# Differential attention in a two-model transformer kernel: three pairs of score banks, and attention maps combined before they are normalized

## The reference, cut to what matters

```python
lam = exp(sum(lam_q1 * lam_k1)) - exp(sum(lam_q2 * lam_k2)) + lam_init
for i in range(S // BLOCK):                      # 4 blocks of 128 queries
    n_k = (i + 1) * BLOCK
    s = einsum('bqhcd,bkhcd->bhcqk', q[:, i*BLOCK:n_k], k[:, :n_k]) * D ** -0.5
    s = where(kpos <= qpos, s, -inf)
    p = softmax(s, axis=-1)                      # two maps, c = 0 and c = 1
    a = p[:, :, 0] - lam * p[:, :, 1]
    outs.append(einsum('bhqk,bkhe->bqhe', a, v[:, :n_k]))
o = rms_norm(concatenate(outs, axis=1), sub_gain) * (1.0 - lam_init)   # EPS = 1e-6 inside the root
```

## Time and profile before

| | us |
|---|---|
| median of three runs | 3162.12 |
| lowest, highest | 3160.61, 3165.22 |
| profiled execution, its own time | 3168.31 |
| its span in the trace | 3166.3 |
| the differential attention in it, from the last projection matmul to the first matmul behind it | 133.7 (1515.7 to 1649.4) |

### The profile page before, as it was taken

One profiled execution on the slowest core, in us unless ns is written; L12 is line 12 of the kernel. 1 busy time (PEld: TensorE's weight loads), 2 busy tenths in 40 slices (PEclk: granted clock), 3 DMA queues, 4 the chain that ended last, 5 costly groups with the idle time before them and its releaser, 6 DMA issues.

```text
span 3166.3 us, 40442 instructions
## 1 busy us (share of the span) xinstructions
PE 2945.4 (93%) x13848; PEld 2410.2 (76%) x13848; DVE 1786.9 (56%) x2233; ACT 1211.5 (38%) x1940; POOL 1097.6 (35%) x474
## 2 busy tenths in 40 slices
PE   5989999999788999999779999999899998899999
PEld 3767778877566888888458888888887897788887
DVE  7565758474795644666566333667265736663333
ACT  2564432233333422244453222366444654332221
POOL 3311444443103444444214444444302441044443
PEclk7999999998898999999889999999899999999999
DMA  5343445442002333333003333332201330033332
GB/s 193 88 146 127 148 133 196 146 146 61 27 1 67 99 96 97 92 95 87 14 14 99 93 93 97 91 94 87 60 1 51 92 90 11 10 97 93 95 98 93
DMA packets 364856, 278.83 MB, mean 88 GB/s; under 512 B 13362, under 2 KB 320947, under 8 KB 363699
## 3 DMA queue, kind: packets, MB, share of 16 engines
q1 hardware_dynamic: 363472, 276.76, 28.5%
q10 hardware_dynamic: 1251, 0.33, 0.0%
HBM read 274.96 MB, written 2.10 MB: 88 GB/s over the span
## 4 chain that ended last, share of the span: by engine, by line
PE 60%; issue 6%; DVE 6%; ACT 2%; POOL 0%; DVEq 0%; ACTq 0%; POOLq 0%
PE banks L943 12%; PE banks L938 12%; PE banks L947 12%; PE banks L895 6%; PE banks L901 6%; PE banks L898 5%; PE banks L870 1%; DVE Z L2278 1%; PE banks L1180 1%; PE banks L1248 1%; DVE small L2233 1%; PE banks L940 1%; ACT tmp L1742 0%; PE banks L1228 0%; DVE head_sums L2347 0%
## 5 line engine op out<-in xcount | busy, mean ns | idle before, releaser
L772 POOL TENSOR_TENSOR w_lo<-w_raw,w_hi 128x1024 fp32r<-128x1024 f32 (+1 forms) x424 | 1045.6, 2466 | 1904.0 <-ACT w_hi L1375 1902.6
L1375 ACT ACTIVATE w_hi<-w_raw 128x1024 fp32r<-128x1024 f32 (+1 forms) x424 | 445.6, 1051 | 1132.6 <-PE banks L947 830.7
L895 PE MATMUL banks<-w_hi,h_hi 128*128 128x512 f32 x960 | 386.9, 403 | 10.5 <-ACT h_hi L1552 7.2
L898 PE MATMUL banks<-w_hi,h_lo 128*128 128x512 f32 x960 | 378.4, 394 | 3.7 <-DVE h_lo L510 3.7
L901 PE MATMUL banks<-w_lo,h_hi 128*128 128x512 f32 x960 | 378.8, 395 | 0.8 <-POOL w_lo L772 0.7
L938 PE MATMUL banks<-h_hi,w_hi 128*128 128x512 f32 x1280 | 340.8, 394 | 10.0 <-ACT h_hi L1559 9.8
L943 PE MATMUL banks<-h_lo,w_hi 128*128 128x512 f32 x1280 | 318.7, 390 | 1.1 <-DVE h_lo L510 1.1
L938 PEld LDWEIGHTS banks<-h_hi,w_hi 128*128 128x128 f32 x1280 | 243.0, 190 | 66.5 <-issue 14.7
L947 PE MATMUL banks<-h_hi,w_lo 128*128 128x512 f32 x1152 | 284.5, 389 | 0.0
L943 PEld LDWEIGHTS banks<-h_lo,w_hi 128*128 128x128 f32 x1280 | 240.2, 188 | 54.0 <-DVE h_lo L510 4.4
L947 PEld LDWEIGHTS banks<-h_hi,w_lo 128*128 128x128 f32 x1152 | 216.2, 188 | 44.9
(11 more groups left out here) (295 smaller groups left out, 4692.3 us busy)
## 6 DMA issues: line engine op xcount, KB each, us to landing
w_raw<-in_m_w_up SPq DMA_DIRECT2D x64, 512.0 KB, 3.9
w_raw<-in_m_w_down SPq DMA_DIRECT2D x64, 512.0 KB, 3.4
Z<-in_ada_w SPq DMA_DIRECT2D x48, 512.0 KB, 4.8
w_raw<-in_kv_w SPq DMA_DIRECT2D x48, 512.0 KB, 3.7
w_raw<-in_ffn_w_gate SPq DMA_DIRECT2D x44, 512.0 KB, 3.8
w_raw<-in_ffn_w_up SPq DMA_DIRECT2D x44, 512.0 KB, 3.8
tmp<-in_ada_w SPq DMA_DIRECT2D x32, 512.0 KB, 4.7
w_raw<-in_ffn_w_down SPq DMA_DIRECT2D x32, 512.0 KB, 3.4
```

The lines of the kernel that those rows point to most:

```text
L772: pool.tensor_tensor(wlo[j][:, 0:n], raw[j][:, 0:n], whi[j][:, 0:n], ALU.subtract).then_inc(s_wlo, 1)
L895: pe.matmul(t, hh, wh, start=k == 0, stop=False)
L898: pe.matmul(t, hl, wh, start=False, stop=False)
L1375: act.activation(whi[par][:, 0:kc * P], raw[par][:, 0:kc * P], ACT.Copy).then_inc(s_whi, 1)
```

## The change

- **Banks and order.** `diff_scores` takes three pairs of banks (0 to 5). TensorE issues scores(0) and scores(1) ahead of the loop and scores(s + 2) in iteration s, ahead of turn_map(s - 3). The wait in scores(s) is for the exponentials of slot s-3, so scores(s + 2) waits for those of slot s-1. VectorE does neg_max(s + 1) in iteration s, ahead of combine(s - 1). ScalarE's loop still does take_map(s - 3) and then probs(s); its scale moves to the first slot of the next head, ahead of take_map, and y_high to the third slot, behind probs.
- **One bank for transposed maps.** All maps are turned into bank 6 (before: 4 and 5 in turn), so turn_map(s) waits until map s-1 is taken. The mean square goes into bank 6 too (before: bank 7), so mean_square waits until the map just turned has been taken, and the next turn_map waits for the Ln that reads it. Values go into bank 7 (before: 6). mean_square stands behind turn_map in its iteration.
- **Combination.** The first map plus the second times a ratio, -lambda l1/l2, where l1 and l2 are the row sums: a reciprocal and a scalar_tensor_tensor on 128x1 and one scalar_tensor_tensor on the map (before: a reciprocal on 128x2 and two operations on the map). The map is left larger by l1; since it is normalized by its mean square afterwards, only EPS has to be scaled: VectorE computes 128 EPS l1^2 once a head (`scale_eps`, 128x4), and TensorE adds it into the mean square with four float32 matmuls of 128 columns a head.
- **Start of the stage.** ScalarE makes the high parts of head 0, VectorE zeroes the unused halves of head 0's key tiles and makes its low parts; GpSimd zeroes those of head 1 and makes the high parts of heads 1 to 7. TensorE waits for GpSimd's zeroing at slot 4 only.

The diff, cut to its core (a line of "..." marks what is left out):

```diff
 def diff_scores(s, c):
-    return bank[2 * (s % 2) + c]
+    return bank[2 * (s % 3) + c]
...
+def diff_eps(s, n=1):
+    return sums8[:, 28 + s % 8:28 + s % 8 + n]
...
     def diff():
-        for h in range(8):
+        for h in range(1, 8):
+            pool.wait_ge(e["high_parts"], past(3 * h))
             pool.wait_ge(e["scores"], past(NB * (h - 1)))
             pool.tensor_copy(q_hi[h % 2], zt(h)).then_inc(e["high_parts"], 1)
             for c, (r, t) in enumerate(zip(HALF, k_hi)):
...
+        if kind == "diff":
+            todo = [qk[64:128, 5 * S:6 * S], qk[64:128, 7 * S:8 * S], qk[0:64, 9 * S:10 * S], qk[0:64, 11 * S:12 * S]]
...
         def scores(s):
...
             pe.wait_ge(e["low_parts"], past(3 * h + 3))
-            pe.wait_ge(e["probs"], past(2 * s - 2))
+            if s == NB:
+                zero_rows_in(4)
+            pe.wait_ge(e["probs"], past(2 * s - 4))
             qh, ql = (t[h % 2][:, b * P:n] for t in (q_hi, q_lo))
             for c in range(2):
...
         def turn_map(s):
...
             pe.wait_ge(e["combined"], past(s + 1))
-            pe.wait_ge(e["taken"], past(s - 1))
+            pe.wait_ge(e["taken"], past(s))
+            pe.wait_ge(e["log_mean"], past((s + BEHIND - NB) // NB))
             for kb in range(b + 1):
-                mm = pe.transpose(bank[4 + s % 2][:, kb * P:(kb + 1) * P], diff_probs(s, 0)[:, kb * P:(kb + 1) * P], ident)
+                mm = pe.transpose(bank[6][:, kb * P:(kb + 1) * P], diff_probs(s, 0)[:, kb * P:(kb + 1) * P], ident)
             mm.then_inc(e["turned"], 1)
...
         def values(h):
...
             for kb in range(NB):
-                mm = pe.matmul(bank[6][:, kb * P:S], zt(16 + h)[:, kb * P:(kb + 1) * P], zt(24 + kb)[:, kb * P:S],
+                mm = pe.matmul(bank[7][:, kb * P:S], zt(16 + h)[:, kb * P:(kb + 1) * P], zt(24 + kb)[:, kb * P:S],
                                start=kb == 0, stop=kb == NB - 1, skip_group_check=True)
             mm.then_inc(e["values_added"], 1)
...
         def mean_square(h):
             pe.wait_ge(e["squares"], past(h + 1))
-            pe.wait_ge(e["log_mean"], past(h))
-            pe.matmul(bank[7], ones, zt(28), start=True, stop=True).then_inc(e["mean_square"], 1)
+            pe.wait_ge(e["taken"], past(min(NB * h + 2 * NB - BEHIND, DIFF_SLOTS)))
+            pe.wait_ge(e["eps_scaled"], past(h + 1))
+            pe.matmul(bank[6], ones, zt(28), start=True, stop=False, skip_group_check=True)
+            for s in range(NB * h, NB * h + NB):
+                _, b = diff_slot(s)
+                mm = pe.matmul(bank[6][:, b * P:(b + 1) * P], diff_eps(s).to_broadcast([P, P]), ident, start=False, stop=s == NB * h + NB - 1, skip_group_check=True)
+            mm.then_inc(e["mean_square"], 1)
+        scores(0)
+        scores(1)
         for s in range(DIFF_SLOTS + BEHIND):
-            if s < DIFF_SLOTS:
-                scores(s)
+            if s + 2 < DIFF_SLOTS:
+                scores(s + 2)
             h, i = divmod(s, NB)
-            if i == NB - 1 and h:
-                mean_square(h - 1)
             if s >= BEHIND:
                 turn_map(s - BEHIND)
+                if i == NB - 1 and h:
+                    mean_square(h - 1)
                 if i == (BEHIND - 1) % NB and h:
                     values(h - 1)
         mean_square(7)
...
         def probs(s):
...
             act.wait_ge(e["neg_max"], past(s + 1))
             act.wait_ge(e["turned"], past(s - 3))
+            act.wait_ge(e["eps_scaled"], past(h - 1))
             for c in range(2):
-                act.activation(diff_probs(s, c)[:, 0:n], diff_scores(s, c)[:, 0:n], ACT.Exp, bias=diff_small(s, 0)[:, c:c + 1],
-                               accum_out=diff_small(s, 1)[:, c:c + 1]).then_inc(e["probs"], 1)
+                act.activation(diff_probs(s, c)[:, 0:n], diff_scores(s, c)[:, 0:n], ACT.Exp, bias=diff_neg_max(s)[:, c:c + 1],
+                               accum_out=diff_sums(s)[:, c:c + 1]).then_inc(e["probs"], 1)
...
         def scale(h):
...
-            act.activation(zt(29), bank[7], ACT.Ln, bias=eps, scale=1.0 / P).then_inc(e["log_mean"], 1)
+            act.activation(zt(29), bank[6], ACT.Ln, scale=1.0 / P).then_inc(e["log_mean"], 1)
...
+        q_hi, _, k_hi, _ = parts("diff")
+        act.activation(q_hi[0], zt(0), ACT.Copy).then_inc(e["high_parts"], 1)
+        for r, t in zip(HALF, k_hi):
+            act.activation(t[0][r, :], zrows(r, 8), ACT.Copy).then_inc(e["high_parts"], 1)
         for s in range(DIFF_SLOTS + BEHIND):
             h, i = divmod(s, NB)
             if i == NB - 1 and h:
                 square(h - 1)
+            if i == 0 and h >= 2:
+                scale(h - 2)
             if s >= BEHIND:
                 take_map(s - BEHIND)
             if s < DIFF_SLOTS:
                 probs(s)
-            if i == NB - 1 and h:
-                scale(h - 1)
-            if i == 1 and h >= 2:
+            if i == 2 and h >= 2:
                 y_high(h - 2)
...
+        def first_parts():
+            for par in range(2):
+                rows = qk[HALF[1 - par], (4 + 4 * par) * S:(8 + 4 * par) * S].rearrange("p (t n) -> p t n", n=2 * S)[:, :, 0:S]
+                dve.memset(rows.bitcast(F32), 0.0)
+            low_q(0)
+            for c in range(2):
+                low_k(0, c)
         def neg_max(s):
...
         def combine(s):
             h, b = diff_slot(s)
             n = (b + 1) * P
             first, second = (diff_probs(s, c)[:, 0:n] for c in range(2))
-            inv = diff_small(s, 2)
+            ratio, inv = diff_ratio(s)
+            l1, l2 = (diff_sums(s)[:, c:c + 1] for c in range(2))
             dve.wait_ge(e["probs"], past(2 * s + 2))
-            dve.wait_ge(e["combined"], past(s - 3))
-            dve.reciprocal(inv, diff_small(s, 1)).then_inc(e["inverted"], 1)
+            dve.wait_ge(e["combined"], past(s - 1))
+            dve.reciprocal(inv, l2).then_inc(e["inverted"], 1)
             dve.wait_ge(e["inverted"], past(s + 1))
-            dve.tensor_scalar(second, second, inv[:, 1:2], lamv, ALU.mult, ALU.mult).then_inc(e["second_scaled"], 1)
-            dve.wait_ge(e["second_scaled"], past(s + 1))
-            dve.scalar_tensor_tensor(first, first, inv[:, 0:1], second, ALU.mult, ALU.subtract).then_inc(e["combined"], 1)
+            dve.scalar_tensor_tensor(ratio, inv, minus_lam, l1, ALU.mult, ALU.mult).then_inc(e["ratio"], 1)
+            dve.wait_ge(e["ratio"], past(s + 1))
+            dve.scalar_tensor_tensor(first, second, ratio, first, ALU.mult, ALU.add).then_inc(e["combined"], 1)
+        def scale_eps(h):
+            l1 = diff_sums(NB * h, NB).rearrange("p (s c) -> p c s", c=2)[:, 0, :]
+            dve.wait_ge(e["probs"], past(2 * NB * h + 2 * NB))
+            dve.wait_ge(e["mean_square"], past(h - 1))
+            dve.scalar_tensor_tensor(diff_eps(NB * h, NB), l1, P * EPS, l1, ALU.mult, ALU.mult).then_inc(e["eps_scaled"], 1)
...
-            dve.scalar_tensor_tensor(ytile[:, :], bank[6], subg, zt(30), ALU.mult, ALU.mult).then_inc(e["normed"], 1)
+            dve.scalar_tensor_tensor(ytile[:, :], bank[7], subg, zt(30), ALU.mult, ALU.mult).then_inc(e["normed"], 1)
...
-        low_q(0)
-        low_k(0, 0)
-        low_k(0, 1)
+        first_parts()
+        neg_max(0)
         for s in range(DIFF_SLOTS + 1):
             h, i = divmod(s, NB)
-            if s < DIFF_SLOTS:
-                neg_max(s)
+            if s + 1 < DIFF_SLOTS:
+                neg_max(s + 1)
             if s:
                 combine(s - 1)
-            if i == 0 and h >= 2:
+            if i == 0 and h:
+                scale_eps(h - 1)
+            if s == 0:
+                low_q(1)
+                low_k(1, 0)
+            if i == 0 and h < 7:
+                low_k(h + 1, 1)
+            if i == 1 and h >= 2:
                 sub_norm(h - 2)
-            if i == 1 and h < 7:
-                low_q(h + 1)
-            if i >= 2 and h < 7:
-                low_k(h + 1, i - 2)
-            if i == 2 and h >= 2:
+            if i == 2 and h < 6:
+                low_q(h + 2)
+            if i == 3 and h < 6:
+                low_k(h + 2, 0)
+            if i == 3 and h >= 2:
                 sub_low(h - 2)
+        sub_norm(6)
         sub_low(6)
         sub_norm(7)
         sub_low(7)
```

More of the change, by code:

```diff
@@ L136, in program @@
         small = sb("small", [P, 64])
-        lamv = small[:, 0:1]
+        minus_lam = small[:, 0:1]
         m2 = small[:, 48:48 + 4 * GROUPS]
@@ L414, in program @@
                         ("high_parts", "low_parts", "values_in", "block_scores", "reduced", "neg_max", "diagonal", "scores", "probs", "values_added", "inverted", "output", "output_high", "output_low", "max_spread", "sink_or_denominator", "squares_or_taken")}
```

(27 more changed lines are left out.)

6 lines of the change are left out of this document (3 added, 3 removed).

## The result

The changed kernel takes 3193.44 us (median of 4 runs, 3188.40 to 3196.59) against 3163.67 us for the kernel before (4 runs, 3160.61 to 3166.82): ratio 1.0091, 95% interval 1.0074 to 1.0108. It is slower, by 29.8 us between the medians; the forecast was +19.5 us and 3181.6 us, with a range of 3164 to 3194. The profiled execution took 3196.59 us, with a span of 3194.8.

What follows compares the result with a forecast made beforehand. No engine is full, so waits bound the stage. Start -2.8, first eight slots +3.5, five middle heads +19.0 and tail -0.2 give +19.5 us on the median 3162.1: 3181.6 us, range 3164 to 3194.

Steps and rivals of the forecast that it cites:

- The order closes a chain of one lap per slot: TensorE and ScalarE wait on each other every slot; laps sum to 15.7 us a head against 13.66, +9.0 in five heads.
- the sign of being right: Copies wait for transposes and scores for exponentials in nearly every slot, stops near 2 us, values over 4 us in most heads.
- The clock falls once a head: TensorE drops to its lower clock level in every head, 2.0 us each; five heads with laps and falls: +19.0 us.
- The first eight slots: Stage's opening slots, 26.93 us before: 28.4 by laps, +1.5, and +3.5 us with one clock fall.
- Start: Stage start, 8.70 us before: ScalarE casts beside VectorE's zeroing, so 5.9 us from the last projection matmul, -2.8 us.
- Added matmuls: Four matmuls of 128 columns a head on TensorE, with the mean square: 0.9 us, bounds 0 to 2.2.
- Tail: End of the stage, 28.57 us before: 24.4, or 28.4 with two clock falls, -0.2 us.
- The clock holds: Rival: the same laps in the stage without clock falls, +3.5 us, 3165.6 us; chance 0.15.
- It falls twice a head, or once but for double length: Rival: 2 us more in five heads and the first eight slots, +31.5 us, 3193.6 us; chance 0.15.
- The lead survives: Rival: exponentials finish before TensorE reaches scores(s+2), so TensorE's work decides, 11.7 us a head; -17.5 us, 3144.6; chance 0.10.
- Nothing much moves: Rival: part of the ring is unseen slack, and the time stays within 5 us; chance 0.05.

Runs made afterwards that it cites:

- filler: The changed kernel plus five unread bf16 matmuls of 512 columns into bank 6 at the places where TensorE would stop; 3169.7 us.
- norm_fill2: The changed kernel with turn_map(s-3) ahead of scores(s+2), sub_norm a slot earlier, and three overwritten matmuls into bank 7 ahead of the values; 3149.6 us.
- turn_first_norm: The changed kernel with turn_map(s-3) ahead of scores(s+2) on TensorE, and sub_norm, sub_low and y_high each a slot earlier; 3161.8 us.
- probs_first: The changed kernel with ScalarE doing probs(s) ahead of take_map(s-3), TensorE's order unchanged; 3163.8 us.
- old_order: The changed kernel with banks, waits and order of the kernel before, keeping the change's start, combination and EPS matmuls; 3164.3 us.

## Why the prediction was right, and where it was off

- **The order closes a chain of one lap per slot: right.** The predicted laps, 3.53, 2.99, and 15.7 a head, measured 3.55 (1611.90 to 1615.45), 2.94 (1597.22 to 1600.16) and 15.49 where the clock held (filler). Scores wait for exponentials in two slots of a head (14 waits in the stage), not in nearly every slot as the sign of being right had it: in the other two slots the transposes, the values and the mean square come between. Cutting the chain at either end takes back 18 to 30 us; leaving it and moving sub_norm takes back nothing.
- **The clock falls once a head: right, but mis-sized.** This is the term that kept the forecast 10 us short. The step "its price is 1.70 to 2.21 by these rows: I take 2.0" was taken from falls that hit the values alone (and the larger of them, at 1628.67, came behind a stop of 1.73 us, not 1.56). Here the clock falls in the stop of 1.69 us, ahead of the scores of 512 keys (1600.16), which then take 3.18 us to the transposes in place of 1.76, and the values follow at the lower level. Against 15.5, heads of 18.2 and 19.4 us make the price 2.7 and 3.9. The five heads from 1559.58 to 1653.01 took 93.4 us, against the forecast 88.5.
- **The first eight slots:** 34.9 us up to scores(10) in place of 30.4 (28.4 and one fall). The mean clock there is 0.66: it was at the lower level for two thirds of the time, and beside the slow first scores I had priced one fall. In filler the same stretch takes 28.8 us, near the 28.4, so it is again the clock and not the laps.
- **Start:** 6.40 us against 9.08, -2.7 as predicted (-2.8). The memset without a row took 0.91 us, the 0.9 of the estimate.
- **Added matmuls:** 1611.09 to 1611.90, 0.81 us, estimated 0.9. **Tail:** 163.29 less 6.40, 34.89 and 93.43 is 28.6 us, as before, and near the predicted 28.4 with two falls; both of its values were slow (4.64 and 4.12 us).
- **The sum:** -2.7 + 8.0 + 23.9 + 0 = +29.2 us. The forecast's terms were -2.8, +3.5, +19.0, -0.2. What is missing is the clock in both middle terms, 9.4 us together. The measured 3193.4 us lies at the very edge of the range, 3164 to 3194. That it came within 0.2 us of the 3193.6 of two falls is luck: by that sum the heads would have added 29.0 us and the first eight slots 5.5, against 23.9 and 8.0, and the median before was 1.5 us higher when it was taken again with the result.
- **The rivals.** "The clock holds" is false for the change; filler shows its laps, and a stage 4.7 us over before, against its +3.5. "It falls twice a head, or once but for double length" came nearest, by time (+31.5) and by what happened: one fall that lasts longer, over scores and values, with slow scores as its argument said. "The lead survives" is false for the order as written. Its price, 11.7 us a head, is near what the same parts reach once the order is mended (12.4), and its 3144.6 us is not far from norm_fill2's 3149.6. "Nothing much moves" is false at +29.8.
- Why the heads alternate between 18.2 and 19.4 us stays open. The trace shows where the difference lies: in the head from 1597.22 the clock is back at the upper level at 1606.5, within the values; in the one from 1577.86 only at 1589.4, in the scores behind them, though the stops ahead are the same 2.01 and 1.69 us.

## What to carry to other kernels

Buffers and lookahead have to be counted together: with three buffers and a lookahead of two, the wait for a free buffer is for the work just before, and every instruction queued behind it inherits that wait. Put the instruction with the tight wait last in its turn on its engine, or keep one buffer in hand. When a wait has gone, read what became late next, and where short stops line up on TensorE, price them with the clock, by all the work that comes behind the stop and not by its first instruction alone.

## What the runs showed of the hardware

- TensorE's clock fell behind stops of 2.01 and 1.69 us with 1.26 us of work between them (1597.22 to 1598.48, granted clock 1.00) in all five middle heads: the scores of 512 keys start at 1600.16 at the lower level (mean granted clock 0.50 from there to 1604.12). Five matmuls in each of those stops kept it at the upper level through whole heads and made the kernel 21 to 24 us faster. The Trainium skill, "TensorE: Matmul & The Clock Gate", Part 1, ties the lower level to an engine that stood idle; here no stop in the head was longer than 2.01 us.
- The same stops don't always bring the same level. In turn_first_norm stops of 0.83 and 0.85 us were followed by values at the lower level in one head and at the upper level in the next; in probs_first a stop of 1.48 us and three of 0.25 to 0.73 in each of five heads left the granted clock at 1.00 throughout (1553.10 to 1620.75).
- The Ln took 0.60 us without a bias tile (1612.18) and 0.70 with one, on the same 128x512. In the change it also reads another bank, but old_order has it without the bias and from bank 7 as before, and there it took 0.60 too in all eight heads, so it goes with the bias and not with the bank:

```profile
...
1558.50 0.60 ACT L1785 ACTIVATE Z<-banks 128x512 f32<-128x512 f32 x1
...
```
